# Routing of a mixture of experts: raw rows turned, routing products inside the next projection tile, frame numbers summed in parts

## What is computed

```python
x = x + mix @ w_out
h = rmsnorm(x, g_ffn)
g_logits = h @ w_group + b_group                       # 4 groups
p_top, g_top = top_k(softmax(g_logits), 1)
e_logits = (einsum('nd,dge->nge', h, w_er) + b_er)[arange(n), g_top]
e_val, e_top = top_k(e_logits, 2)                      # 2 of the group's 8 experts
gate = softmax(e_val) * p_top
x = x + sum over the 2 experts of gate * ((silu(h @ w_gate[e]) * (h @ w_up[e])) @ w_down[e])
y = rmsnorm(x, g_final)
```

## Time and profile before

| what | value |
|---|---|
| median of the runs shown | 1325.03 us (1321.36 to 6504.04, 3 runs) |
| the profiled execution, its own time | 1323.67 us |
| its span, first to last instruction | 1321.9 us |
| PE busy | 1164.5 us (88%) |
| DVE busy | 845.4 us (64%) |
| ACT busy | 684.4 us (52%) |
| POOL busy | 266.0 us (20%) |
| mean granted PE clock | 0.946 of full speed |

### The profile page before, as it was taken

The page is one execution under the profiler, slowest core; times in us unless marked ns, Lnnn a source line. Parts: engine busy times, 40 slices in busy tenths (PEclk is TensorE's granted clock), DMA queues, the critical chain, the costliest instruction groups (busy, mean ns, idle before and its releaser), DMA issues. The chain is left out here.

```text
span 1321.9 us, 17956 instructions
## 1 busy us (share of the span) xinstructions
PE 1164.5 (88%) x6478; PEld 957.7 (72%) x6478; DVE 845.4 (64%) x1681; ACT 684.4 (52%) x1159; POOL 266.0 (20%) x297
## 2 busy tenths in 40 slices
PE   6999789999999898999999869999299999999930
PEld 5666458787878797898989648887278888888820
DVE  3325877787787784623222352354689999999947
ACT  3314648676777623333333441211188888888712
POOL 2333002424242300000000000000113333334112
PEclk9999879999999998999999989998599999999965
DMA  6304121030302032142432623014199999999756
GB/s 231 53 15 101 39 56 37 3 102 3 102 3 80 3 101 84 49 144 72 116 100 73 227 66 134 33 49 170 66 390 383 396 392 397 388 393 391 282 200 257
DMA packets 129056, 204.27 MB, mean 155 GB/s; under 512 B 17316, under 2 KB 102468, under 8 KB 116676
## 3 DMA queue, kind: packets, MB, share of 16 engines
q1 hardware_dynamic: 114996, 177.88, 37.7%
q0 software_dynamic: 12672, 20.47, 4.8%
q10 hardware_dynamic: 1296, 4.72, 0.9%
HBM read 181.50 MB, written 34.37 MB: 163 GB/s over the span
## 5 line engine op out<-in xcount | busy, mean ns | idle before, releaser
L1741 DVE TENSOR_TENSOR place<-place,place 128x2048 fp32r<-128x2048 f32 x64 | 146.2, 2287 | 9.9 <-ACT place L1182 9.9
L1999 PE MATMUL psum<-place,place 128*128 128x512 f32 x288 | 124.4, 432 | 7.0 <-issue 4.0
L1013 ACT ACTIVATE place<-place,place 128x768 uint8<-128x768 f32 (+3 forms) x128 | 125.6, 983 | 7.6 <-DVE place L1377 7.6
L1182 ACT CAST place<-place 128x2048 fp32r<-128x2048 f32 x64 | 122.1, 1912 | 0.0
L2001 PE MATMUL psum<-place,place 128*128 128x512 f32 x288 | 114.8, 399 | 0.0
L2000 PE MATMUL psum<-place,place 128*128 128x512 f32 x288 | 114.4, 397 | 0.0
L2242 PE MATMUL psum<-place,place 128*128 128x512 f32 x256 | 106.4, 416 | 0.0
L2244 PE MATMUL psum<-place,place 128*128 128x512 f32 x256 | 101.4, 396 | 0.0
L2243 PE MATMUL psum<-place,place 128*128 128x512 f32 x256 | 100.6, 393 | 0.0
L855 POOL TENSOR_TENSOR place<-place,place 128x1 f32<-128x1 f32 x9 | 4.9, 550 | 432.6 <-DVE place L1682 432.6
L1975 PE MATMUL psum<-place,place 128*128 128x256 f32 x288 | 85.8, 298 | 1.8 <-ACT place L1035 1.8
(11 more groups left out here) (308 smaller groups left out, 3023.3 us busy)
## 6 DMA issues: line engine op xcount, KB each, us to landing
place<-in_w_gate SPq DMA_DIRECT2D x32, 1024.0 KB
place<-in_w_up SPq DMA_DIRECT2D x32, 1024.0 KB
place<-in_w_down SPq DMA_DIRECT2D x32, 1024.0 KB, 10.5
place<-in_w_in SPq DMA_DIRECT2D x28, 512.0 KB, 5.8
place<-expert_out SPq DMA_DIRECT2D x9, 1024.0 KB, 12.7
place<-in_cache_attn_k SPq DMA_DIRECT2D x32, 256.0 KB, 3.1
place<-in_cache_attn_v SPq DMA_DIRECT2D x32, 256.0 KB, 3.2
place<-in_x_prompt SPq DMA_DIRECT2D x3, 1536.0 KB, 8.9
```

Of the source, the lines that this page charges most:

```text
L1013: last = nc.scalar.activation(reached[j], score[j], ACT.Sign, bias=pivot.bitcast(F32)[:, j:j + 1], scale=-1.0, accum_out=minus[:, j - BY_A ...
L1182: nc.scalar.copy(w_gu_hi[e % 2][:, :, ks, :], w_gu[e % 3][:, :, ks, :]).then_inc(w_hi_done, 1)
L1741: nc.vector.tensor_tensor(w_gu_lo[e % 3][:, :, ks, :], w_gu[e % 3][:, :, ks, :], w_gu_hi[e % 2][:, :, ks, :].bitcast(F32), ALU.subtract).t ...
L1999: nc.tensor.matmul(bank(4 + b), hT_hi[:, k, rows], w_hi[:, k, :], start=k == 0, stop=False)
```

## The change

**Projection loop.** PE transposes the raw rows x1 of the tile before, not the scaled h2, and does so in the midst of a tile: 24 products, transposes of tile t - 1, 12 products, routing products of tile t - 1, 12 products. The scale is applied elsewhere: w_route is multiplied once by g_ffn (a new load, g_cols), and the logits by the row's 1/rms when they are read from PSUM (`logits`). Rank products of a part come two tiles behind its end, and frame products of a part another tile later.

**ACT** copies the turned frames of tile t - 1 at the head of iteration t. The first exponential of a part stands at the end of iteration `end`, the second at the head of iteration `end + 1`. For the last part they stand beside the two halves of expert 0's split.

**DVE.** `choose` ends with the picks' copy, then the gap and a copy of hot for PE. The gates are a function of their own, `gates_of`, behind `ranks`. `ranks` compares with the rank itself, without the three conversions to a row inside a block. Main frames are summed over the parts (`main_frames`) and written by `place_frames` for the 32 main blocks, before gates and counts.

**Overflow blocks** (18 of 50) get their frame numbers behind expert 0: DVE forms rows and table anew after rows_lo(0), PE multiplies after gate_up(0) (`over_frames`), and DVE writes them in front of rows_lo(1). frames_done goes to 2 with the main blocks and to 4 with these.

**SP** issues gate and up of expert 0 ahead of the stores of h2, and holds the down weights of expert 1 and all of expert 2 until frames_done is 4.

The core of the diff (of PE's part only the new side):

```diff
+            sp.dma_start(g_cols, i_["g_ffn"][0].rearrange("(p k) -> p k", k=KD)).then_inc(route_in, 16)
...
+            load_gate_up(0)
...
-            load_gate_up(0)
             load_down(0)
...
-            for n in range(2):
-                sp.wait_ge(x6_in[n], 16)
+            sp.wait_ge(frames_done, 4)
             load_down(1)
...
-            for t in range(T + 1):
-                if t < T:
-                    if t >= 2:
-                        act.wait_ge(h2_out[t % 2], 16 * (t // 2))
-                        act.wait_ge(h2tr_ps, t - 1)
-                    act.wait_ge(x1_done, t + 1)
...
+            def turned_frames(t):
+                act.wait_ge(h2tr_ps, t + 1)
+                if t >= 2:
+                    act.wait_ge(rt_ps, t - 1)
+                nc.scalar.copy(h2T[t % 2], bank(4, 0, D).rearrange("p (k n) -> p k n", k=KD)).then_inc(h2T_done, 1)
+            def group_exp(x, start, end):
+                act.wait_ge(exp_ready, 2 * x + 1)
+                nc.scalar.activation(t_g[1][:, start:end], t_g[0][:, start:end], ACT.Exp).then_inc(exp_done, 1)
+            def expert_exp(x, start, end):
+                act.wait_ge(exp_ready, 2 * x + 2)
+                nc.scalar.activation(t_small[6][:, start:end], t_small[5][:, start:end], ACT.Exp).then_inc(exp_done, 1)
+            for t in range(T):
+                for x, (start, end) in enumerate(PARTS):
+                    if t == end + 1:
+                        expert_exp(x, start, end)
+                if t >= 1:
+                    turned_frames(t - 1)
+                if t >= 2:
+                    act.wait_ge(h2_out[t % 2], 16 * (t // 2))
...
+                nc.scalar.activation(h2[t % 2], x1[:, t, :], ACT.Square, accum_out=ssq5[:, t:t + 1]).then_inc(ssq_done, 1)
                 if t + 2 < T:
                     high_mix(t + 2)
-                if t >= 1:
-                    act.wait_ge(h2tr_ps, t)
-                    if t >= 3:
-                        act.wait_ge(rt_ps, t - 2)
-                    nc.scalar.copy(h2T[(t - 1) % 2], bank(4, 0, D).rearrange("p (k n) -> p k n", k=KD)).then_inc(h2T_done, 1)
                 for x, (start, end) in enumerate(PARTS):
-                    if t == min(end + 1, T):
-                        act.wait_ge(exp_ready, 2 * x + 1)
-                        nc.scalar.activation(t_g[1][:, start:end], t_g[0][:, start:end], ACT.Exp).then_inc(exp_done, 1)
-                        act.wait_ge(exp_ready, 2 * x + 2)
-                        nc.scalar.activation(t_small[6][:, start:end], t_small[5][:, start:end], ACT.Exp).then_inc(exp_done, 1)
+                    if t == end:
+                        group_exp(x, start, end)
+            turned_frames(T - 1)
 
             def rows_hi(e):
...
             def gate_silu(e):
                 act.wait_ge(gu_ps, e + 1)
+                if e == 0:
+                    act.wait_ge(frames_done, 4)
                 if e >= 2:
...
             gate_up_hi(0, 0)
+            group_exp(len(PARTS) - 1, *PARTS[-1])
             gate_up_hi(0, 1)
+            expert_exp(len(PARTS) - 1, *PARTS[-1])
             act.wait_ge(frames_done, 1)
...
-                tt(gap[:, tiles], top_logit[:, 1, tiles], top_logit[:, 0, tiles], ALU.subtract).then_inc(exp_ready, 1)
                 L(v, tt(picked[:, tiles], hot[:, 0, tiles], hot[:, 1, tiles], ALU.add))
...
                 nc.vector.tensor_copy(picked_pe[:, tiles], picked[:, tiles]).then_inc(picks_done, 1)
+                tt(gap[:, tiles], top_logit[:, 1, tiles], top_logit[:, 0, tiles], ALU.subtract).then_inc(exp_ready, 1)
+                L(v, nc.vector.tensor_copy(hot_pe[:, :, tiles], hot[:, :, tiles]))
+            def gates_of(x, start, end):
+                tiles = slice(start, end)
...
-                L(v, nc.vector.tensor_copy(row_bits[:, :, tiles], rank[:, :, tiles]))
-                L(v, ts(row_bits[:, :, tiles], row_bits[:, :, tiles], P - 1, None, ALU.bitwise_and))
-                L(v, nc.vector.tensor_copy(slot_row[:, :, tiles], row_bits[:, :, tiles]))
                 for j in range(2):
                     for t in range(start, end):
-                        last = ts(at_row(j, t), C("column"), slot_row[:, j, t:t + 1], C("row")[:, T * j + t:T * j + t + 1], ALU.is_equal, ALU.mult)
+                        last = ts(at_row(j, t), C("column"), rank[:, j, t:t + 1], C("row")[:, T * j + t:T * j + t + 1], ALU.is_equal, ALU.mult)
                 last.then_inc(rows_done, 1)
...
+            def main_frames(x):
+                v.wait_ge(frames_ps, x + 1)
+                got = bank(7, T * NE + NE * x, NE)
+                if x == 0:
+                    L(v, nc.vector.tensor_copy(main_values, got))
+                else:
+                    L(v, tt(main_values, main_values, got, ALU.add))
+            def place_frames(to, values):
+                second_row = e_try.rearrange("p t n -> p (t n)")[:, 0:to.stop - to.start]
+                L(v, ts(second_row, values, float(NTOK - NO_ROW), float(-NTOK), ALU.is_ge, ALU.mult))
+                nc.vector.scalar_tensor_tensor(block_frames[:, to], values, float(NO_ROW), second_row, ALU.add, ALU.add).then_inc(frames_done, 1)
+                return ts(block_rows[:, to], values, float(NO_ROW), None, ALU.add)
...
+            def logits(t):
+                v.wait_ge(rt_ps, t + 1)
+                nc.vector.scalar_tensor_tensor(route[:, t, :], bank(6, 0, 36), rstd5[:, t:t + 1], b_route, ALU.mult, ALU.add).then_inc(rt_done, 1)
+            for t in range(T):
+                if t >= 1:
+                    logits(t - 1)
...
+                for x, (start, end) in enumerate(PARTS):
+                    if t == end:
+                        choose(x, start, end)
+                    if t == end + 1:
+                        ranks(x, start, end)
+                        gates_of(x, start, end)
+                    if t == end + 2:
+                        main_frames(x)
...
+            logits(T - 1)
+            choose(len(PARTS) - 1, *PARTS[-1])
+            ranks(len(PARTS) - 1, *PARTS[-1])
+            gate_up_lo(0, 0)
+            main_frames(2)
+            place_frames(slice(0, NE), main_values).then_inc(frames_done, 1)
+            gates_of(len(PARTS) - 1, *PARTS[-1])
+            gate_up_lo(0, 1)
             L(v, nc.vector.tensor_copy(e_cnt, bank(5, 0, NE)))
             L(v, tt(t_thr, e_cnt.unsqueeze(2).broadcast_to([P, NE, 8]), C("thr").unsqueeze(1).broadcast_to([P, NE, 8]), ALU.is_gt))
             L(v, nc.vector.reduce_sum(e_blk, t_thr, AX))
...
 
+            v.wait_ge(h2_out[0], 16 * ((T + 1) // 2))
+            v.wait_ge(h2_out[1], 16 * (T // 2))
+            rows_lo(0)
...
-            tt(at_block, slot_block.unsqueeze(3).broadcast_to([P, 2, T, NBLK]),
-               C("blocks").unsqueeze(1).unsqueeze(1).broadcast_to([P, 2, T, NBLK]), ALU.is_equal).then_inc(slots_done, 1)
+            L(v, ts(row_bits, slots, P - 1, None, ALU.bitwise_and))
+            L(v, nc.vector.tensor_copy(slot_row, row_bits))
+            for j in range(2):
+                for t in range(T):
+                    last = ts(at_row(j, t), C("column"), slot_row[:, j, t:t + 1], C("row")[:, T * j + t:T * j + t + 1], ALU.is_equal, ALU.mult)
+            last.then_inc(rows_done, 1)
+            over_blocks = C("blocks")[:, NE:NBLK].unsqueeze(1).unsqueeze(1).broadcast_to([P, 2, T, NOVER])
+            tt(at_over, slot_block.unsqueeze(3).broadcast_to([P, 2, T, NOVER]), over_blocks, ALU.is_equal).then_inc(slots_done, 1)
...
+            v.wait_ge(frames_ps, len(PARTS) + 1)
+            place_frames(slice(NE, NBLK), bank(5, 0, NOVER)).then_inc(frames_done, 1)
...
+            def part_frames(x, start, end):
+                pe.wait_ge(rows_done, x + 1)
+                for j in range(2):
+                    for t in range(start, end):
+                        last = nc.tensor.matmul(bank(7, T * NE + NE * x, NE), at_row(j, t), hot_pe[:, j, t, :],
+                                                start=j == 0 and t == start, stop=j == 1 and t == end - 1)
+                last.then_inc(frames_ps, 1)
+            def turn_frames_x1(s):
+                pe.wait_ge(x1_done, s + 1)
+                if s:
+                    pe.wait_ge(h2T_done, s)
+                for k in range(KD):
+                    last = nc.tensor.transpose(bank(4, k * P, P), x1[:, s].rearrange("p (d k) -> p k d", k=KD)[:, k, :], ident)
+                last.then_inc(h2tr_ps, 1)
+            def route_frames(s):
+                if s:
+                    pe.wait_ge(rt_done, s)
+                else:
+                    pe.wait_ge(route_scaled, 1)
+                pe.wait_ge(h2T_done, s + 1)
+                for k in range(KD):
+                    last = nc.tensor.matmul(bank(6, 0, 36), h2T[s % 2][:, k, :], w_route[:, k, :], start=k == 0, stop=k == KD - 1)
+                last.then_inc(rt_ps, 1)
+            def out_part(t, m, c):
...
             pe.wait_ge(ov_read, T * AH)
+            for t in range(T):
                 if t >= 2:
```

(23 more changed lines are left out.)

161 lines of the change are left out of this document (58 added, 103 removed).

## The result

| | kernel before | changed kernel |
|---|---|---|
| median of the runs | 1328.45 us (4 runs, 1321.36 to 6504.04) | 1343.96 us (4 runs, 1343.88 to 1349.13) |
| ratio | | 1.0135, interval 1.0105 to 1.0165 |
| profiled execution | 1323.67 us, span 1321.9 | 1349.13 us, span 1347.3 |

The forecast was 1341.4, range 1330 to 1350. The change cost 1 to 2%. To compare profiles, the span is cut at marks that every run has: S, the first product of the output projection; W, the end of its last work (six frame products included, where they stand there); P, the end of the instruction that writes block_frames; the first down product; and G, the start of the transposes of expert 4's rows, from where PE runs without a gap in the expert loop.

What follows compares the result with a forecast made beforehand. The prediction took PE to bound the kernel, with gains only where PE stands idle. Its terms, 6.0 + 16.6 - 14.0 + 9.1 = +17.7 us on 1323.67, gave 1341.4 us, range 1335 to 1348 (wider: 1330 to 1350).

Steps and rivals of the forecast that it cites:

- Term B: Projection, tiles 4 and 7: PE waits for ACT's copy queued behind the second exponential, 8.3 us per stall; +16.6 us.
- Term D: First experts, behind P: overflow work on DVE and the late load of expert 2's weights delay the first down product; +9.1 us.
- Term C: Tail, projection's end to P: early routing and fewer steps before the main frame numbers shorten it; -14.0 us.
- Term A: Output projection: transposes, routing, rank and frame products moved in front of its end, none hidden on PE; +6.0 us.
- R1: Projection: no stalls on ACT's copy, because the picks are ready in time; no change, 1324.8 us; chance 0.07.
- R2: First experts: only Term D fails, as DVE absorbs the slots' work; 1332.3 us; chance 0.12.
- R3: Expert stage: paced by the weight stream, not PE, so all ends 22.2 us later; 1345.9 us; chance 0.15.
- R4: Projection: light blocks amid dense tiles, with the stalls, keep PE at its lower clock; 23 us more, 1364; chance 0.04.

Runs made afterwards that it cites:

- a1: Changed kernel with ACT's copy of the turned frames put in front of the second exponential in tiles 4 and 7; ratio 1.0015 to the kernel before.
- a8: a6 with SiLU no longer waiting for the overflow numbers; only ACT's split of expert 0's down weights waits, for PE's products; S to G 192.50 us, one execution.
- a6: a4 with DVE writing the overflow blocks' frame numbers behind the first half of expert 1's weight split; ratio 0.9935 to the kernel before.
- a7: Changed kernel with PE's routing products moved to the end of the tile in tiles 4 and 7; S to G 209.06 us, one execution.
- a0: Changed kernel run again, unedited, as the measure for the other runs; ratio 1.0156 to the kernel before.
- a5: Changed kernel without the overflow blocks' frame numbers, expert 2's weights held until expert 0's gate and up products are done; S to G 217.06 us, one execution.
- a3: a1 with the split undone: all 50 blocks' frame numbers formed in the tail, early routing kept; ratio 0.9996 to the kernel before.
- a4: Changed kernel with both the edit of a1 and that of a2; ratio 0.9918 to the kernel before.
- a2: Changed kernel with overflow rows and tables in memory no weight buffer covers, so held weights load after the first two gathers; ratio 1.0134 to the kernel before.
- a9: a1 with ACT's and DVE's splits of expert 0's hidden rows put before the first half of expert 2's weight split; ratio 0.9981 to the kernel before.
- a10: Changed kernel with the edits of a1, a2, a6, a8 and a9 together; ratio 0.9929 to the kernel before.

## Why the prediction was right or wrong

The time (1343.96) lies in the range, within 2% as forecast, and the case is the forecast's own: the waits are where it put them. On the stretch that the change touches, S to G, the sum was 3.9 us short: +17.7 against +21.6. That the time is only 2.6 us off is in part luck: B, D and what was left out came 6.3 us dearer, C 2.5 cheaper, and the medians of the two kernels are 18.9 us apart where the marks say 21.6.

- **Term A**, +6.0: a1 isolates it at 6.1. Right.
- **Term B**, +16.6: the place and the releaser are as told, and a1 shows the cause. The gaps were 5.84 and 5.68 instead of 6.3. The mis-sized part is "2.0 us lost" to the clock. It was 3.85 on average. I had taken it from a restart with dense products, which were back at their pace after 4.4 us. Here the restart is with routing products; they took 3.60 instead of 1.87, and what stood behind was still slow: up to some 9 us after the first restart (863.46), up to 923.64 and so 7.0 us after the second (916.67). The first down products, which are dense, bear out that this kind of restart makes the difference: behind gaps of 2.58 to 10.84 us (a8, a6, a7, the changed kernel, a0, a1, a5) the stretch from them to G was 1.3 to 2.4 us longer than the 12.37 of the kernel before, and the 10.84 us of a5 cost 1.3. No run has both kinds behind the same gap. B is 19.2.
- **Term C**, -14.0: it measured -16.5. Two steps were too dear. I took the transposes to start 1.6 us behind the projection's end, but DVE's addition runs beside the six frame products, and they start 0.74 behind W (1.32 in a3, which has no such products). And the last routing block took 2.39 instead of 3.5, since the clock had not all fallen; in a1 it took 3.60, and W to P was 21.05. So 1.2 of the 16.5 are clock and not the order of the work; why it fell later here is not shown.
- **Term D**, +9.1: 10.4. The chain of reasons holds: release at P + 21.3 (forecast 21.5), split 4.6 us in front of the product (4.7). (The terms behind the load, 1.9, 2.2 and 0.4, add up to 36.0 and not to the 36.2 that the sum has.) The mis-sized step is the load: "8.0 us, with some 2 us to start and land", 10 in all, took 11.6 to ACT's split. SP issues seven loads within 3.1 us (980.93 to 984.00, the last two are expert 3's), where the sum counted three. In a4 the same four go out first (946.79 on) and the next one only 13.4 us later; there the last of expert 2's gate and up weights landed 9.9 us after its issue at 947.64, 10.7 after the first. So 0.7 of the missing 1.6 is there without the three further loads; that these three took the other 0.9 is argued from the order and the rate (403 GB/s in 990 to 1000). DVE alone makes 6.1 (a2), where I had 6.5.
- **The sum left out** what the low clock does behind D's gap: 2.35 between the first down product and G.
- **Two readings of rows** were wrong and cost nothing. The earlier trace rows has both halves of the first split behind P, not one. And between the first gather and the first down product PE waits once more than said, 2.63 us in front of 957.67; the changed kernel has the same 2.63 at 968.97.
- **R1** fell (both gaps are there), **R2** too (D is there in full). **R3**: the load is the wait that ends last at the first down product (ACT's 7.14 us, and a5) and in a9 once more at expert 3, but not from G on: PE is busy 100.00 of 100 us there, and all runs take 334.7 to 336.0 us from G to the end. **R4** fell: dense products between the blocks stay at 0.24 us, and the clock falls only at the gaps or right behind them. The prediction had put R4 beside what the Trainium skill says in "TensorE: Matmul & The Clock Gate" (A second HAM failure mode), that frequent short idles between groups of products make the clock swing. This projection has hardly any idle time, so it doesn't test that; it shows that transposes, routing and rank products in the midst of dense work left the granted clock where it was. One window over nearly all of a1's projection (columns as in the earlier trace rows) has it at 1.00 with PE busy 122.52 of 123 us:

```profile
794.00:917.00 123.00, 122.52 (x632) 102.30 (x630) 51.01 (x129) 24.52 (x35) 4.38 (x8) 1.00 0.20 78
```

## What to carry to other kernels

In an engine's written order, a small instruction that needs the end of a long chain must not stand in front of one whose input is ready and on which the critical engine waits; look at each moved block for what now stands ahead of it, not only for what it does. Taking work off the chain in front of a mark pays only if what is put behind it holds back nothing: here 8.7 us gained came back as 8.9, 4 to 5 us of it from scratch memory that shared its place with a weight buffer and so delayed a load (a2, a4); once the waits behind P were shortened one after the other, P to the first down product was as short as before (a10). And where two delays lie side by side, an experiment that removes one shows little; remove them in turn and together.

## What the runs showed of the hardware beyond that

**Where the granted clock falls, and when.** A gap of 3.0 us (a7) cost 1.86 us of clock, gaps of 5.7 to 5.8 us cost 3.85 on average, all with light products behind them. Gaps of 0.43 to 1.59 us in front of the first down product (a2, a4, a3, the kernel before) left the stretch to G at 12.37 to 12.41; one of 2.58 us (a8) made it 13.99, with a granted clock of 0.50 from 972 to 974. In a7 the routing products behind the gap still ran at the higher level (1.95 for what takes 1.87), and the clock fell only in the window of 860 to 862, some 2 us after the restart, with PE busy all the while. So the price of a gap has to be looked for behind its end too, not only at it.

**Nearly the same code takes 788 to 802 us up to S.** The change adds next to nothing there: a7 has it and reached S at 787.90, earlier than the kernel before. Rows of the windows over the first 200 us of four profiled executions; the third number from the right, PEclk, is 0.94, 0.92, 0.91 and 0.89. First the kernel before (S = 788.91), then a4 (790.71), the changed kernel (792.74) and a0 (798.60):

```profile
0.00:200.00 200.00, 167.02 (x760) 116.58 (x761) 101.02 (x174) 85.25 (x141) 49.33 (x68) 0.94 0.32 85
```

```profile
0.00:200.00 200.00, 166.55 (x744) 117.12 (x745) 98.69 (x168) 81.93 (x134) 47.80 (x65) 0.92 0.29 77
```

```profile
0.00:200.00 200.00, 165.63 (x725) 116.31 (x726) 98.22 (x166) 80.79 (x132) 47.77 (x65) 0.91 0.28 73
```

```profile
0.00:200.00 200.00, 167.17 (x714) 117.39 (x714) 94.73 (x152) 79.94 (x131) 45.98 (x63) 0.89 0.28 72
```

In these four, the lower the clock at the start, the later S. It is not the whole of it: a2 has 0.93 and S at 793.40, and the four runs with 0.89 lie between 798.40 and 802.44. Why it differs from run to run stays open. The 14 us are two thirds of what the change cost on its own stretch. The spread fits that the medians without the execution of 6504.04 us differ by 18.9 us where the marks say 21.6, while the fastest runs of both (1343.88 and 1321.36) are 22.5 apart; and that a4's median is 11.6 us below that of the kernel before, where the marks say 3.9 and the fastest runs (1317.78 and 1322.73) are 4.95 apart. Marks around the change measure an effect of a few us in one profile; medians over whole runs needed it to be larger.
